# Other PSUM banks, rectifiers on ScalarE and a later down projection in a fused two-model transformer kernel

## The reference, cut to what matters

```python
# model 1
x = x + gt_m * hybrid_mixer(h)     # RG-LRU (recurrent) half and gated linear attention half
x = x + gt_f * f                   # layer 0: swiglu, width 2816; layer 1: 8 experts, top 2
# model 2
x = x + gt_m * mixer(h)            # 8-head attention, 8-head mLSTM, two branches, w_out
x = x + gt_f * (gelu(a) * val) @ w_down   # a, val: halves of a causal conv over h @ w_up
return rms_norm(x, final_g)
```

## Time and profile before

| what | us |
| --- | --- |
| three runs: median (lowest, highest) | 2198.56 (2198.36, 2201.16) |
| the profiled execution, its own time | 2195.71 |
| its span in the profile | 2193.9 |
| busy in the span: PE, PEld, DVE, ACT | 2134.3, 1920.0, 1749.8, 1228.6 |
| granted clock of TensorE, mean | 0.989 of full |

### The profile page before, as it was taken

One profiled execution on the slowest core, in us unless ns is written; L12 is line 12 of the kernel. 1 busy time (PEld: TensorE's weight loads), 2 busy tenths in 40 slices (PEclk: granted clock), 3 DMA queues, 4 the chain that ended last, 5 costly groups with the idle time before them and its releaser, 6 DMA issues.

```text
span 2193.9 us, 33378 instructions
## 1 busy us (share of the span) xinstructions
PE 2134.3 (97%) x13865; PEld 1920.0 (88%) x13865; DVE 1749.8 (80%) x1903; ACT 1228.6 (56%) x1367; POOL 54.0 (2%) x101
## 2 busy tenths in 40 slices
PE   5999999999999999999999999999999999999998
PEld 4989999987888888888888899888999998889998
DVE  5998777878899998989999977777767677756665
ACT  3724444736777777777767755542555455324554
POOL 1000000000000000000000000000000000000000
PEclk8999999999999999999999999999999999999999
DMA  9887985747999999999999967738555376345552
GB/s 313 316 306 283 327 313 183 247 155 285 380 379 358 373 374 381 348 371 379 369 366 381 377 226 215 250 102 279 179 191 180 109 197 204 103 135 173 175 191 78
DMA packets 339039, 578.55 MB, mean 264 GB/s; under 512 B 48098, under 2 KB 208954, under 8 KB 326594
## 3 DMA queue, kind: packets, MB, share of 16 engines
q1 hardware_dynamic: 324604, 475.34, 63.3%
q0 software_dynamic: 13824, 100.67, 11.8%
q10 hardware_dynamic: 454, 0.34, 0.1%
HBM read 575.26 MB, written 1.05 MB: 263 GB/s over the span
## 4 chain that ended last, share of the span: by engine, by line
PE 81%; DVE 10%; ACT 4%; DMA 4%; issue 2%; DVEq 0%; ACTq 0%; SPq 0%; POOL 0%; POOLq 0%
PE bank L597 79%; DVE w_low L2129 2%; ACT arena L1578 2%; DMA ada_in<-in_ada_w 2%; DVE ada_acc L2137 1%; DMA ring<-in_ffn_w 1%; DVE arena L2137 1%; DVE arena L2129 1%; PE bank L1337 1%; DMA ring<-in_moe_w 1%; DVE arena L2623 1%; ACT mix_hi L1578 1%; ACT L1578 1%; DVE arena L2601 0%; DVE arena L2414 0%
## 5 line engine op out<-in xcount | busy, mean ns | idle before, releaser
L2129 DVE TENSOR_TENSOR w_low<-ring,moe_w_hi 128x2048 fp32r<-128x2048 f32 x264 | 594.8, 2285 | 12.9 <-ACT moe_w_hi L1578 8.8
L1578 ACT ACTIVATE moe_w_hi<-ring 128x2048 fp32r<-128x2048 f32 x264 | 506.3, 1918 | 167.1 <-DMA ring<-in_moe_w 125.0
L597 PE MATMUL bank<-h_hi,w_hi 128*128 128x256 f32 x1056 | 258.5, 284 | 1.8 <-ACT h_hi L1578 0.9
L597 PE MATMUL bank<-h_hi,w_low 128*128 128x256 f32 x1056 | 257.8, 281 | 0.0
L597 PE MATMUL bank<-mix_h_hi,mix_hi 128*128 128x256 f32 x800 | 231.9, 293 | 9.7 <-ACTq L1575 7.4
L597 PE MATMUL bank<-mix_h_hi,w_low 128*128 128x256 f32 (+2 forms) x848 | 239.3, 285 | 0.0
L597 PE MATMUL bank<-h_low,mix_hi 128*128 128x256 f32 x800 | 213.9, 283 | 0.0
L2137 DVE SCALAR_TENSOR_TENSOR ada_acc<-ada_in,c_col,ada_acc 128x2048 f32<-128x2048 f32 x84 | 197.2, 2347 | 16.1 <-DMA ada_in<-in_ada_w 11.3
L597 PEld LDWEIGHTS bank<-h_hi,w_hi 128*128 128x128 f32 x1056 | 198.7, 188 | 3.5 <-issue 2.1
L597 PEld LDWEIGHTS bank<-h_hi,w_low 128*128 128x128 f32 x1056 | 200.2, 190 | 0.1
L1578 ACT ACTIVATE arena<-bank 128x512 f32<-128x512 f32 (+2 forms) x171 | 90.1, 527 | 185.9 <-PE bank L597 181.9
(11 more groups left out here) (219 smaller groups left out, 4540.8 us busy)
## 6 DMA issues: line engine op xcount, KB each, us to landing
ring<-in_moe_w SPq DMA_DIRECT2D x264, 1024.0 KB, 6.5
ada_in<-in_ada_w POOLq DMA_DIRECT2D x96, 1024.0 KB, 7.4
ring<-in_w_in SPq DMA_DIRECT2D x56, 1024.0 KB, 5.5
ring<-in_ffn_w_up SPq DMA_DIRECT2D x44, 1024.0 KB, 7.7
ring<-in_ffn_w SPq DMA_DIRECT2D x33, 1024.0 KB, 8.4
ring<-in_ffn_w_down SPq DMA_DIRECT2D x22, 1024.0 KB, 4.9
ring<-in_w_out SPq DMA_DIRECT2D x16, 1024.0 KB, 5.3
ring<-in_w_br_mla SPq DMA_DIRECT2D x4, 1024.0 KB, 5.1
```

The source lines that it names most:

```text
L597: ins = nc.tensor.matmul(out, lhsT, rhs, start=start, stop=stop, skip_group_check=shared)
L1578: return nc.scalar.activation(out, in_, f, **kw)
L2129: return nc.vector.tensor_tensor(out, a, b, op)
```

## The change

It has five parts.

1. **`mixer1`, banks.** The scores go to banks 0 and 7 in place of 7 and 0 (DVE reads in that order too), the first half of g to bank 0 in place of 4, and the two norm sums to banks 4 and 1 in place of 0 and 1.
2. **`mixer2`, attention.** The projections beside attention take banks 5 and 6 in turn.
3. **`mixer2`, mLSTM.** `log_weights` leaves DVE. ACT makes max(m - a, 0) itself, with two Relu functions a head, straight from the bank and with -a as the bias (DVE now writes -a, counted by `atok_sb`); before heads 2 to 7 it waits until the weights two heads back have been used. DVE's mask multiplies only the two diagonal blocks, 256 columns in place of 384.
4. **The last feed-forward's end** (`late`). PE runs no down projection after up 20; after up 21 it runs downs 19 and 20, then 21. The last rows of w_down are rounded into a weight buffer that is free by then (`w_hi[2]`).
5. **Roots and final scaling.** A one-column square root (`root_table`) after each of the three feed-forwards whose norm follows on ACT without a mixer between. In the final scaling ACT multiplies only the even blocks of x; DVE multiplies the odd ones, each one residual later (`odd_block`).

The diff's changed lines (a line "..." where unchanged ones lie between, up to twelve columns of indent taken away; the semaphores' list, where `w_arg` goes and `atok_sb` and `final_odd` come, is left out, and so is the loop at L2604 that called `log_weights`):

```diff
@@ -124,6 +124,7 @@
+BESIDE_BANKS = (5, 6, 5, 6, 5, 6)
@@ -831,11 +832,11 @@
-    for b in (7, 0):
+    for b in (0, 7):
...
-        for hh, b in enumerate((7, 0)):
+        for hh, b in enumerate((0, 7)):
@@ -850,7 +851,7 @@
-    project_bank(("g", li, 0), 4)
+    project_bank(("g", li, 0), 0)
@@ -874,9 +875,9 @@
-    for half in range(2):
-        fill(half)
-        mm(bank[half][:, :], ones, M1["osq"][:, half * 512:(half + 1) * 512], inc="headsum_psum")
+    for half, b in enumerate((4, 1)):
+        fill(b)
+        mm(bank[b][:, :], ones, M1["osq"][:, half * 512:(half + 1) * 512], inc="headsum_psum")
@@ -1056,11 +1057,11 @@
-            project_bank(("gmla", li, step - 1), 6)
+            project_bank(("gmla", li, step - 1), BESIDE_BANKS[step - 1])
...
-            project_bank(("gml", li, 0), 6)
+            project_bank(("gml", li, 0), BESIDE_BANKS[4])
...
-            project_half(("gml", li, 1), 6, step - 6)
+            project_half(("gml", li, 1), BESIDE_BANKS[5], step - 6)
@@ -1207,7 +1208,7 @@
-def ffn(kind, li, f0, beside=None):
+def ffn(kind, li, f0, beside=None, late=False):
@@ -1225,17 +1226,20 @@
+            if fb2 == 1 and not (late and f == FFN_FB - 1):
+                owed.append(2)
+        if f == FFN_FB and beside:
+            beside()
+        behind = () if late and f == FFN_FB - 2 else (f - 2, f - 1) if late and f == FFN_FB - 1 else (f - 1,)
+        for g in behind if f else ():
+            c, fb2 = divmod(g, 2)
+            pe.wait_ge(s["down_lo"], f0 + g + 1)
+            rows_hi = (down_hi_ffn if kind == "w" else down_hi_conv)[g % 2]
+            if late and g == FFN_FB - 1:
+                rows_hi = w_hi[2]
+            down_split(plan[(kind + "2", li, c)][0], fb2, g % 2, rows_hi, g == 0, f == FFN_FB)
...
-                owed.append(2)
-        if f >= 1:
-            c, fb2 = divmod(f - 1, 2)
-            if f == FFN_FB and beside:
-                beside()
-            pe.wait_ge(s["down_lo"], f0 + f)
-            down_split(plan[(kind + "2", li, c)][0], fb2, (f - 1) % 2,
-                       (down_hi_ffn if kind == "w" else down_hi_conv)[(f - 1) % 2], f == 1, f == FFN_FB)
-            if fb2 == 1:
-                owed.append(1)
+                owed.append(3 if late and g == FFN_FB - 3 else 1)
@@ -1530,7 +1534,7 @@
-ffn("u", 1, F0["conv1"])
+ffn("u", 1, F0["conv1"], late=True)
@@ -1542,6 +1546,7 @@
+    need("final_odd")
@@ -1632,15 +1637,17 @@
-def down_rows_high(kind, li, f, f0):
+def down_rows_high(kind, li, f, f0, last=None):
...
-    if f >= 2:
+    if last is not None:
+        act.wait_ge(s["up_done"], f0 + f - 1)
+    elif f >= 2:
...
-    func((down_hi_ffn if kind == "w" else down_hi_conv)[f % 2][:, :],
+    func((down_hi_ffn if kind == "w" else down_hi_conv)[f % 2][:, :] if last is None else last,
@@ -1652,6 +1659,10 @@
+def root_table():
+    func(small[:, 255:256], ones[:, 0:1], ACT.Sqrt)
@@ -1770,11 +1781,11 @@
-    for half in range(2):
+    for half, b in enumerate((4, 1)):
...
-        tell(func(M1["ostd"][:, half * 512:(half + 1) * 512], bank[half][:, :], ACT.Sqrt,
-                  scale=1.0 / P, bias=EPS), "headstd_sb", half)
-    for half, b in enumerate((4, 5)):
+        tell(func(M1["ostd"][:, half * 512:(half + 1) * 512], bank[b][:, :], ACT.Sqrt,
+                  scale=1.0 / P, bias=EPS), "headstd_sb", b)
+    for half, b in enumerate((0, 5)):
@@ -1862,8 +1873,9 @@
+            b = BESIDE_BANKS[unit]
...
-            tell(func(region(unit * 512, 512), bank[6][:, :], ACT.Copy), None, 6)
+            tell(func(region(unit * 512, 512), bank[b][:, :], ACT.Copy), None, b)
@@ -1876,9 +1888,15 @@
+    need("atok_sb")
...
-        need("w_arg")
+        need("mb_psum")
+        if head >= 2:
+            act.wait_ge(s["scores_sb"], 4 + 8 * li + head - 1)
+        b = head % 2
...
+        func(wm[:, 0:T], bank[b][:, 0:T], ACT.Relu, bias=small[:, 112 + head:113 + head])
+        tell(func(wm[:, T:384], bank[b][:, P:T], ACT.Relu, bias=small[:, 120 + head:121 + head]), None, b)
@@ -2055,7 +2073,7 @@
-        down_rows_high("u", li, f, f0)
+        down_rows_high("u", li, f, f0, w_hi[2][:, 0:DM] if li and f == FFN_FB - 1 else None)
@@ -2069,6 +2087,7 @@
+root_table()
@@ -2080,20 +2099,21 @@
+root_table()
...
+root_table()
...
-    for k in (2 * j, 2 * j + 1):
-        ins = func(h[:, k, :], x[:, k, :], ACT.Copy, scale=gain[:, k:k + 1])
-    ins.then_inc(s["final_x"], 1)
+    func(h[:, 2 * j, :], x[:, 2 * j, :], ACT.Copy, scale=gain[:, 2 * j:2 * j + 1])\
+        .then_inc(s["final_x"], 1)
@@ -2199,13 +2219,13 @@
-def down_rows_low(kind, li, f, f0):
+def down_rows_low(kind, li, f, f0, last=None):
...
-    hi = (down_hi_ffn if kind == "w" else down_hi_conv)[f % 2]
-    tt(w_low[:, slot, rows_of], ring[:, slot, rows_of], hi[:, :].bitcast(F32), ALU.subtract)
+    hi = (down_hi_ffn if kind == "w" else down_hi_conv)[f % 2][:, :] if last is None else last
+    tt(w_low[:, slot, rows_of], ring[:, slot, rows_of], hi.bitcast(F32), ALU.subtract)
@@ -2364,7 +2384,7 @@
-    for half, b in enumerate((7, 0)):
+    for half, b in enumerate((0, 7)):
@@ -2520,7 +2540,7 @@
-    tell(nc.vector.tensor_copy(small[:, 112:128], bank[5][:, 0:16]), None, 5)
+    tell(ts(small[:, 112:128], bank[5][:, 0:16], -1.0, ALU.mult), "atok_sb", 5)
@@ -2573,22 +2593,15 @@
-    def log_weights(head):
-        need("mb_psum")
-        b = head % 2
-        wm = M2["wm"][:, (head % 2) * 384:(head % 2) * 384 + 384]
-        ts(wm[:, 0:T], bank[b][:, 0:T], small[:, 112 + head:113 + head], ALU.subtract, 0.0, ALU.max)
-        tell(ts(wm[:, T:384], bank[b][:, P:T], small[:, 120 + head:121 + head], ALU.subtract,
-                0.0, ALU.max), "w_arg", b)
...
-        settle(tt(wm, wm, const[:, C_CAUSAL:C_CAUSAL + 384], ALU.mult))
+        diagonal = wm.rearrange("p (b t) -> p b t", b=3)[:, 0:3:2, :]
+        settle(tt(diagonal, diagonal,
+                  const[:, C_CAUSAL:C_CAUSAL + P].unsqueeze(1).to_broadcast([P, 2, P]), ALU.mult))
@@ -2602,8 +2615,6 @@
-        for head in (2 * pair, 2 * pair + 1):
-            log_weights(head)
@@ -2890,7 +2901,7 @@
-        down_rows_low("u", li, f, f0)
+        down_rows_low("u", li, f, f0, w_hi[2][:, 0:DM] if li and f == FFN_FB - 1 else None)
@@ -2903,7 +2914,16 @@
-    residual((4, 5, 6, 7), 40, "down_part")
+    gain = vcol[:, 3, PACK2["final"]:PACK2["final"] + KB]
+    def odd_block(j):
+        if li and j:
+            k = 2 * j - 1
+            ts(h[:, k, :], x[:, k, :], gain[:, k:k + 1], ALU.mult).then_inc(s["final_odd"], 1)
+    residual((4, 5, 6, 7), 40, "down_part", odd_block)
+    odd_block(KB // 2)
```

More of the change, by code:

```diff
@@ L92 @@
 ri_psum rope_ready scores_psum silu_done sp_exp states_sb stored u_ready units_used up_done v_sb
-vcol_ready w_arg w_exp wout_psum x_psum x_ready ycat_ready yla_sb yml_ready z_br
+vcol_ready w_exp wout_psum x_psum x_ready ycat_ready yla_sb yml_ready z_br
     zeroed headsq_sb headsum_psum outgate_sb scores_sb z_loggate
@@ L96 @@
 moe_hid moe_turned moe_ht_hi moe_ht_lo moe_hx_psum moe_hx_hi moe_hx_lo moe_picked moe_prep moe_spread_t
-moe_spread moe_added dn_down moe_y moe_y_low routing_psum logits_sb dn_psum z_up mla_sb half_used down_part rows_hi later_in small_zero final_x final_scale out_sb_high norm_mean2
+moe_spread moe_added dn_down moe_y moe_y_low routing_psum logits_sb dn_psum z_up mla_sb half_used down_part rows_hi later_in small_zero final_x atok_sb final_scale final_odd out_sb_high norm_mean2
 two_diag two_factor
```

## The result

The changed kernel takes 2185.97 us in the median of 4 runs (2182.73 to 2187.28), the kernel before 2198.46 (2197.33 to 2201.16): a ratio of 0.994, with a 95% interval of 0.9928 to 0.9951, or 12.5 us less (10.8 to 15.8). Forecast were 2184.3 and 14.3 less, the range from 2180.5 to 2190.5.

A forecast was written before the change was run, and what follows sets the result against it. PE, 97% busy, bounds the kernel, so only its ended idle times count: 1.5 + 3.8 + 6.0 - 0.3 + 3.25 = 14.25 us off the median of 2198.56 gives 2184.3, range 2180.5 to 2190.5.

The forecast's parts named there:

- what PE gains earlier it waits here: First model, layer 0's norm: DVE's conditioning products end the residual regardless, so the new banks give 0, ends 0 and 1.5.
- a new stall at half clock: Anywhere in the changed kernel: PE newly stalling with the clock at 0.50 would make the prediction wrong; no size given.
- Rival C: Wait before mLSTM's last branch grows to about 1.6, half clock follows, 1.7 us lost per mixer: 2187.7 us, chance 0.08.
- the three waits: Attention's projections in each mixer: PE's idles of 0.81, 0.40 and 1.33 for ACT's copy give 0.97, 0.56 and 0.4.
- X + 0.16: Any PE wait: wholly ending a recorded idle of X gains this, as matmuls start 0.12 apart but are recorded with 0.28.
- The third wait: Attention's projections: after the 1.33 idle for ACT's copy, DVE's low part is late next; 0.4 gained, not 1.49.
- the +5.1 and the +6.5 of the working: mLSTM pair: ACT finishes both heads' Relus and exponentials 5.1 us after the pair's start, late case 6.5.
- Rival B: mLSTM: DVE's chain stays the limit, or ACT fills to 9.2; 2 x 2.7 lost, 2189.7 us, chance 0.11.
- the place named: After second model's first feed-forward: the early root's table load delays ACT's high part, DVE's lows and the residual: -0.3.
- DVE as the limit at 1.4 per j: Kernel's end: DVE's residuals and one scaled block set 1.4 per j, outputs 8.7 after the first down: 1.2 gained.
- without the idle I expect full clock: Kernel's end: ending the 1.90 idle before down 21 also avoids the 3.41 us at clock 0.50.
- rival D: mLSTM: Relu outside Exp's table makes each head load two tables of 1.28; slower, 2205.9 us, chance 0.04.

The follow-up runs named there:

- the later wait: Against the changed kernel, DVE waits for the output gate's sigmoid only just ahead of the product with it: 2183.76 us, ratio 0.9942.
- the moved product: Against the changed kernel, DVE's third conditioning product beside attention moves from step 3 to step 4: 2182.94 us, ratio 0.9939.

## Why the prediction was right

The sum was right in its direction and range, with 12.5 measured against 14.3. By its own terms:

- **Part 1**, layer 1: 1.5 forecast, 1.36 to 1.37 measured. **Layer 0** is the step that failed: "what PE gains earlier it waits here. I take 0; the ends are 0 and 1.5". The waiting itself came as forecast: PE was 1.38 earlier from g on, and took 1.39 longer from the norm's first sums to the eight matmuls behind the wait (4.70 in place of 3.31). What the step put at nothing is the clock behind the longer wait. From those eight matmuls to the norm's end four profiles with the old banks take 18.8 to 18.9; with the new ones eight take 19.0 to 19.4 and two 24.5 and 24.7. That is 0.3 lost mostly, 5.7 now and then, 1.4 on average over the ten, of which only two set the size. The lower end should have been below nothing. The prediction also named "a new stall at half clock" as a sign of being wrong: one came, here, and was small enough to leave the sum right. Rival C had the mechanism, at another place: at 1933.00, where it put it, the wait grew to 1.22 only and the clock stayed full.
- **Part 2**: 3.8 forecast, 4.2 measured, by the stretches and by the run that undid it. In the second mixer the three waits gave 1.06, 0.67 and 0.42, for 0.97, 0.56 and 0.4: ending a wait gave some 0.1 more than X + 0.16, and the matmul just behind a wait is recorded with 0.39 and not 0.28. The third wait is held by DVE's low part, as forecast (0.96 left).
- **Part 3**: 6.0 forecast, 5.6 measured, rectifiers and mask together. The first combine gained 0.26 (0.28 forecast), the second and third 1.27 each (1.35), and the fourth and what follows gave each other back (0.40 gained, 0.40 lost). The second exponential was ready at +5.70 in the pair that was worked out (+5.35 in the one shown), between the +5.1 and the +6.5 of the working. Rival B would have left pairs of 10.56; they take 9.31.
- **Part 4**: -0.3 forecast, -0.33 measured, at the place named.
- **Part 5**: 3.25 forecast. Over the twelve profiles with the late order the last 24 downs to the output take 8.9 on average, and with 2.85 for the first 24 the end takes 11.75 against 14.80 before: 3.05. The 14.80 are one profile's; the old order took 15.88 in the run that undid it. DVE as the limit at 1.4 per j held (1.38 at full clock). The step "without the idle I expect full clock" held up to the output in four of the twelve, and in two more the clock fell too late to cost anything (5.3 us behind the last down): these six took 8.45 to 8.46, under the 8.7 forecast. In the other six it fell 3.2 to 4.8 us behind the last down and cost 0.1 to 1.5.

1.36 + 4.2 + 5.6 - 0.33 + 3.05 - 1.4 = 12.5, and 13.6 with layer 0's more frequent 0.3. The median's 12.5 has an interval of 10.8 to 15.8 and holds both, so its agreement with the first to the tenth is luck. The forecast's 14.3 was right by its mechanisms in all parts but layer 0.

No row of before showed Relu under the exponential's table, and that left rival D its chance of 0.04. The rows now show it under two tables with no load of its own. The Trainium skill, "ScalarE: Activation LUTs", section "Table sets: the hidden batching unit", has simple functions in every set; with that the runs agree for these two tables. The Trainium skill, "ScalarE: Activation LUTs", section "Rules for kernel authors", gives relu to VectorE, for being up to about 3 times faster per element in bf16. The tiles here are fp32, and the two engines took the same 0.7 us per head, so that reason did not apply. Moving the rectifiers to ACT, with the smaller mask, took 5.6 us off the time, since DVE ended PE's wait and ACT did not.

## What to carry to other kernels

When one engine is busy for 97% of the time, price a change by the idle times that it ends, each up to what is late next; here that gave every part within 0.5 us but layer 0's. Where the work of the bounding engine is moved ahead of a wait that another engine sets, the wait grows, and a longer wait can cost more than nothing: look at the clock behind it. Scatter of several us per execution hides gains of 1 to 4 us in a median, while the stretch between two numbered matmuls in a profile shows most of them to 0.1.

## What the runs showed of the hardware

The granted clock fell to 0.50 behind layer 0's norm whenever PE had idled 2.19 us there (ten profiles) and not at 1.34 to 1.88 (four); it mostly came back after 3.4 us, and twice only after 13.6. Which of the two comes in a given execution was not settled, nor whether the length of the idle time alone decides. Half clock for 3.4 us cost only 0.3 there; with the old banks PE idles 0.78 for DVE behind the eight matmuls, and in the profiles with the short fall it does not. At the kernel's end, in the sums and transposes behind the last down, it fell while PE still worked without idle (stretches of the changed kernel, columns as in the earlier trace rows):

```profile
2172.90:2176.80 3.90, 3.90 (x38) 3.83 (x36) 3.00 (x8) 2.85 (x7) 0.00 (x0) 1.00 0.01 4
2176.80:2179.50 2.70, 2.70 (x15) 2.45 (x13) 0.30 (x2) 0.61 (x3) 0.00 (x0) 0.50 0.00 0
```

The same matmuls ran through at full clock in other executions of the same kind of end. Whether other work on PE would hold the clock there was not tried.

It fell without idle time at another place too, at the start of the second model's second mixer, in three of the fourteen profiles (one bank beside attention, the later wait, the moved product; at 1818.0, 1810.3 and 1821.4 us). Eight matmuls of only 8 rows each (`gate_rows`) had begun 2.8 to 3.4 us before. Each fall lasted 3.4 us and cost 1.5. In the run with the later wait:

```profile
1810.33:1813.74 3.41, 3.41 (x19) 3.41 (x18) 3.09 (x3) 2.64 (x5) 0.00 (x0) 0.50 1.07 401
```

In the other eleven profiles the same matmuls ran at full clock, so part of what scatters between executions is this.
